# A two-block network on one core: layer norms that read their statistics from PSUM, and a state space stage with groups innermost and tiles taken in turn

## The reference

```python
bu_re = einsum('blgh,gph->lbgp', u, bb_re)          # 64 groups of 16 features, 64 states
bu_im = einsum('blgh,gph->lbgp', u, bb_im)
s_re, s_im = associative_scan(s_t = lbar * s_(t-1) + bu_t)
y = einsum('lbgp,ghp->blgh', s_re, c_re) - einsum('lbgp,ghp->blgh', s_im, c_im)
h = gelu(y + d_skip * x)
z = val(h @ w_glu) * sigmoid(gate(h @ w_glu));  mix = z @ w_out

h = layer_norm(ALPHA * h + mix, g, b)                # (x - mean) * rsqrt(var + eps) * g + b
h = layer_norm(ALPHA * h + swiglu_ffn(h), g2, b2)
```

## Time and profile before

| | |
|---|---|
| median of 3 runs | 2775.85 us (2774.55 to 2780.78) |
| the profiled execution | 2774.27 us, span from first to last instruction 2772.6 us |
| busy | PE 2511.0 us (91%), PEld 2037.5, DVE 1363.1 (49%), ACT 802.0, POOL 377.2 |
| mean granted TensorE clock | 0.966 of full speed |
| DMA | 210.20 MB, mean 76 GB/s |

### The profile page before, as it was taken

How to read it: one execution, slowest core, us unless ns; L and a number is a source line. 1 busy time by engine, 2 the same in 40 slices (tenths; PEclk the granted TensorE clock), 3 DMA queues, 4 the chain that set the end, 5 groups by cost and what they waited for, 6 DMA issues and landing times.

```text
span 2772.6 us, 31672 instructions
## 1 busy us (share of the span) xinstructions
PE 2511.0 (91%) x12367; PEld 2037.5 (73%) x12367; DVE 1363.1 (49%) x1587; ACT 802.0 (29%) x864; POOL 377.2 (14%) x254
## 2 busy tenths in 40 slices
PE   3359979999989998999997989899999998999999
PEld 2258768888868766788885866788787887788887
DVE  7983463333553566433355355554534435544443
ACT  3112232222231452322224245322322233222322
POOL 4920040000310005000032202100022000200000
PEclk9779999999999999999998999999999999999999
DMA  3042212322322001222233210232233220232232
GB/s 60 1 65 61 91 61 91 103 89 83 100 80 91 31 1 61 91 91 91 78 94 90 92 61 16 77 104 91 77 94 91 90 91 16 79 102 91 81 92 84
DMA packets 255936, 210.20 MB, mean 76 GB/s; under 512 B 12612, under 2 KB 253658, under 8 KB 255802
## 3 DMA queue, kind: packets, MB, share of 16 engines
q1 hardware_dynamic: 255018, 207.42, 24.6%
q0 software_dynamic: 848, 1.80, 0.4%
HBM read 204.75 MB, written 2.10 MB: 75 GB/s over the span
## 4 chain that ended last, share of the span: by engine, by line
PE 83%; DVE 10%; issue 2%; ACT 2%; SPq 1%; POOL 1%; DMA 0%; DVEq 0%; POOLq 0%; ACTq 0%
PE psum L753 14%; PE psum L755 14%; PE psum L754 14%; PE psum L784 9%; PE psum L785 8%; PE psum L786 8%; PE psum L868 2%; PE psum L870 2%; PE psum L869 2%; DVE residual L2017 1%; PE psum L739 1%; PE psum L708 1%; POOL tmp_a L523 1%; PE psum L904 1%; PE psum L922 1%
## 5 line engine op out<-in xcount | busy, mean ns | idle before, releaser
L1873 DVE TENSOR_TENSOR w_lo<-w_stage,w_hi 128x2048 fp32r<-128x2048 f32 x203 | 477.5, 2352 | 698.5 <-ACT w_hi L1286 698.5
L1286 ACT CAST w_hi<-w_stage 128x2048 fp32r<-128x2048 f32 x210 | 401.2, 1910 | 1403.1 <-PE psum L755 744.3
L784 PE MATMUL psum<-x_hi,w_hi 128*128 128x512 f32 x944 | 380.9, 403 | 71.8 <-DVE x_lo L2026 40.1
L785 PE MATMUL psum<-x_lo,w_hi 128*128 128x512 f32 x944 | 373.3, 395 | 0.0
L786 PE MATMUL psum<-x_hi,w_lo 128*128 128x512 f32 x944 | 372.6, 395 | 0.0
L753 PE MATMUL psum<-x_hi,w_hi 128*128 128x512 f32 x944 | 367.2, 389 | 0.0
L754 PE MATMUL psum<-x_lo,w_hi 128*128 128x512 f32 x944 | 367.2, 389 | 0.0
L755 PE MATMUL psum<-x_hi,w_lo 128*128 128x512 f32 x944 | 367.2, 389 | 0.0
L753 PE MATMUL psum<-hidden_hi,w_hi 128*128 128x512 f32 x832 | 325.4, 391 | 8.0 <-DVE w_lo L1873 2.9
L754 PE MATMUL psum<-hidden_lo,w_hi 128*128 128x512 f32 x832 | 323.8, 389 | 0.0
L755 PE MATMUL psum<-hidden_hi,w_lo 128*128 128x512 f32 x832 | 323.7, 389 | 0.0
(11 more groups left out here) (377 smaller groups left out, 3152.0 us busy)
## 6 DMA issues: line engine op xcount, KB each, us to landing
w_stage<-in_ffn_w_gu_dram SPq DMA_DIRECT2D x44, 1024.0 KB, 5.0
w_stage<-in_ffn_w_down_dram SPq DMA_DIRECT2D x64, 704.0 KB, 4.5
w_stage<-in_ffn_w_gate_dram SPq DMA_DIRECT2D x22, 1024.0 KB, 5.3
w_stage<-in_ffn_w_up_dram SPq DMA_DIRECT2D x22, 1024.0 KB, 5.3
w_stage<-in_sb_w_qkv_dram SPq DMA_DIRECT2D x12, 1024.0 KB, 5.0
w_stage<-in_od_w_in_dram SPq DMA_DIRECT2D x12, 1024.0 KB, 5.3
w_stage<-in_ev_w_in_dram SPq DMA_DIRECT2D x10, 1024.0 KB, 5.1
w_stage<-in_ssm_w_glu_dram SPq DMA_DIRECT2D x8, 1024.0 KB, 5.6
```

The costliest lines, as they stand in the source:

```text
L784: nc.tensor.matmul(bank[u], hi, xh[:, k, :], start=(k == 0), stop=False)
L785: nc.tensor.matmul(bank[u], hi, xl[:, k, :], start=False, stop=False)
L1286: nc.scalar.copy(whi[:, half, :], wst[:, half, :]).then_inc(whi_done, 1)
L1873: V.tensor_tensor(wlo[:, half, :], wst[:, half, :], whi[:, half, :].bitcast(F32), ALU.subtract).then_inc(wlo_done, 1)
```

## The change

Norms: the mean is no longer copied, and `mean` is bank 5 itself. ACT writes the reciprocal root into bank 6 (`rstd_all`), in the rms norms too. All eight chunks are centred by DVE, so that POOL goes from its sums straight to the last weight split. The order of DVE's steps changes: multiply chunk c, make `x_lo` of chunk c-1, centre chunk c+2. In norm 4 the mean square goes to bank 7.

State space stage: the input is copied unrounded (`x_f`), its `x_lo` is gone, and `ssm_out` takes the residual from `x_f` without rebuilding it. `toe` and `k_rows` are laid out with the group inside the time step, so that each DMA moves one contiguous run per partition. The matmuls of lines 708 and 739 are issued so that consecutive ones go to different tiles (four in turn), those of line 726 so that they alternate between two. Matmuls on different row halves go to different banks: banks are worked on in pairs, and the semaphores of a pair rise together. ACT now waits for all eight of POOL's `cl` rounds before its first copy to `k_rows` (before: ahead of its third), PE for six rounds before the first pair of line 708 and for eight before the second (before: five, six, seven, eight for the four banks).

```diff
+        mean, rstd_all = bank[5], bank[6]
-        mean, mean_sq, variance, rstd_ln = acc, tmp_c[:, 0, :], tmp_c[:, 1, :], tmp_b[:, 1, :]
+        mean_sq, variance, rstd_ln = tmp_c[:, 0, :], tmp_c[:, 1, :], tmp_b[:, 1, :]
-        toe = at("toeplitz", [P, GROUPS, P], hid_at + 36 * KB)
+        toe = at("toeplitz", [P, 4, TAU, 16, GH], hid_at + 36 * KB)
-        k_rows = at("k_rows", [P, 16, P], tmp_at + 8 * KB)
+        k_rows = at("k_rows", [P, TAU, 16, GH], tmp_at + 8 * KB)
+        x_f = at("x_feat", [P, DC, SEQ], xhi_at)
...
-                eng.dma_start(toe[s * GH:(s + 1) * GH, (q // 2) * 32 + q % 2:(q // 2) * 32 + 32:2, s * GH:P],
-                              k_rows[q * 32:q * 32 + GH, :, 0:P - s * GH]).then_inc(done, 16)
+                eng.dma_start(toe[s * GH:(s + 1) * GH, q, s:TAU, :, :],
+                              k_rows[q * 32:q * 32 + GH, 0:TAU - s, :, :]).then_inc(done, 16)
...
-                pool.wait_ge(ln_m2, 2 * n + 2)
-
-                pool.wait_ge(dev_sq, (n + 1) * DC)
-                for c in range(4, DC):
-                    sum_link(nc.gpsimd.tensor_tensor(res[:, c, :], res[:, c, :], mean, ALU.subtract))
                 split_last(n)
...
-            for b in range(4):
-                pe.wait_ge(w_ready, 4 + b + 1)
-                for q in range(4):
+            for b0 in (0, 2):
+                pe.wait_ge(w_ready, 4 + b0 + 2)
+                for swap in range(2):
                     for s in range(4):
-                        g = (q // 2) * 32 + 2 * (b * 4 + s) + q % 2
-                        j, half = g // 2, (g % 2) * 64
                         for ri, w in enumerate((w_re, w_im)):
-                            mm = nc.tensor.matmul(bank[4 + b][q * 32:q * 32 + 32, s * P:(s + 1) * P],
-                                                  bb[half:half + 64, ri, :, j], w[half:half + 64, j, 0:TAU, :], start=(ri == 0), stop=(ri == 1))
-                mm.then_inc(k_done, 1)
+                            for q in range(4):
+                                b = b0 + ((q % 2) ^ swap)
+                                g = (q // 2) * 32 + 2 * (b * 4 + s) + q % 2
+                                j, half = g // 2, (g % 2) * 64
+                                mm = nc.tensor.matmul(bank[4 + b][q * 32:q * 32 + 32, s * P:(s + 1) * P],
+                                                      bb[half:half + 64, ri, :, j], w[half:half + 64, j, 0:TAU, :],
+                                                      start=(ri == 0), stop=(ri == 1))
+                mm.then_inc(k_done, 2)
...
-            for b in range(8):
-                for g, dst in y_parts(b):
-                    j, half = g // 2, (g % 2) * 64
+            for b0 in range(0, 8, 2):
+                for s in range(4):
                     for ri, w in enumerate((w_re, w_im)):
-                        mm = nc.tensor.matmul(dst, states[half:half + 64, 0:NCH, ri, j], w[half:half + 64, j, 1:LAGS, :],
-                                              start=False, stop=(ri == 1), skip_group_check=True)
-                mm.then_inc(y_done, 1)
-                if b >= 3 and b % 2 == 1:
-                    y_features(b - 3)
-                    y_features(b - 2)
+                        for b in (b0, b0 + 1):
+                            for hf in range(2):
+                                g, dst = y_part(b, s, hf)
+                                j, half = g // 2, (g % 2) * 64
+                                mm = nc.tensor.matmul(dst, states[half:half + 64, 0:NCH, ri, j], w[half:half + 64, j, 1:LAGS, :],
+                                                      start=False, stop=(ri == 1), skip_group_check=True)
+                mm.then_inc(y_done, 2)
+                if b0 >= 2:
+                    y_features(b0 - 2)
+                    y_features(b0 - 1)
...
-                nc.scalar.activation(mean_sq, bank[5], ACT.Square).then_inc(ln_m2, 1)
-                nc.scalar.copy(mean, bank[5]).then_inc(ln_m2, 1)
+                nc.scalar.activation(mean_sq, mean, ACT.Square).then_inc(ln_m2, 1)
...
-                nc.scalar.activation(rstd_ln, rstd_ln, ACT.Exp, scale=-0.5).then_inc(act_link, 1)
+                nc.scalar.activation(rstd_all, rstd_ln, ACT.Exp, scale=-0.5).then_inc(act_link, 1)
...
-            for f in range(DC):
-                dve.wait_ge(xhi_done, f + 1)
-                V.tensor_tensor(xlo[:, f, :].rearrange("p (c s) -> p s c", s=TAU),
-                                bank[f][:, :].rearrange("p (s c) -> p s c", s=TAU),
-                                xhi[:, f, :].bitcast(F32).rearrange("p (c s) -> p s c", s=TAU),
-                                ALU.subtract).then_inc(x_ready, 1)
+            V.memset(marks[:, 11:12], 0.0).then_inc(x_ready, DC)
...
+                for c in range(DC):
+                    dve.wait_ge(ln_xc, n * DC + c + 1)
+                    V.tensor_tensor(res[:, c, :], res[:, c, :], rstd_all, ALU.mult).then_inc(ln_n, 1)
+                    if n < 3 and c > 0:
+                        low(c - 1)
+                    if c + 2 < DC:
+                        centre(c + 2)
+                pass_split(n)
+                if n < 3:
+                    low(DC - 1)
```

More of the change, by code:

```diff
@@ L723, in _ @@
             for b in range(8):
[L724 to L726 removed]
+                for s in range(4):
+                    for hf in range(2):
+                        g, dst = y_part(b, s, hf)
+                        nc.tensor.matmul(dst.rearrange("p (t h) -> p t h", h=GH), uu[:, g, :], toe_of(g), start=(s == 0),
+                                         stop=False, skip_group_check=True)
             def y_features(n):
@@ L833, in mean_square @@
                 pe.wait_ge(ln_sq, sq_count(n) + c + 1)
-                nc.tensor.matmul(bank[5], ones_mean[:, :], sq[:, c % 2, :], start=first, stop=last).then_inc(ln_sq_used, 1)
+                nc.tensor.matmul(bank[7 if n == 4 else 5], ones_mean[:, :], sq[:, c % 2, :], start=first,
+                                 stop=last).then_inc(ln_sq_used, 1)
             def norm(n):
@@ L1938, in shift @@
                 for c in range(DC):
-                    V.scalar_tensor_tensor(res[:, c, :], bank[4], -1.0 / (2 * P * (1.0 if c < 4 else ALPHA)), res[:, c, :],
+                    before = x_f[:, c, :] if n == 0 and c >= 4 else res[:, c, :]
+                    V.scalar_tensor_tensor(res[:, c, :], bank[4], -1.0 / (2 * P * (1.0 if c < 4 else ALPHA)), before,
                                            ALU.mult, ALU.add).then_inc(ln_shifted, 1)
```

59 lines of the change are left out of this document (25 added, 34 removed).

## The result

The changed kernel takes **2728.12 us** in the median of 4 runs (2726.96 to 2729.36), the kernel before 2778.32 us in its 4 (2774.55 to 2782.95). The ratio is 0.982, with a 95% interval from 0.980 to 0.984. Forecast were 2724 us and a range from 2715 to 2739. The profiled execution took 2728.07 us, against 2774.27 before, so 46.2 us are to be found between the two traces.

What follows compares the result with a forecast made beforehand. PE was taken to bound the kernel, so its gaps counted. Norms 0 to 2 (22.8 us), norm 3 (7.1) and the state space stage (22.4) sum to 52.3 us off 2774.3, plus 1.6 for the median: 2724 us, range 2715 to 2739.

Steps and rivals of the forecast that it cites:

- Norms 0 to 2: PE's gap of 13.4 us ahead of each of these layer norms' first matmul shrinks by 7.6 us, 22.8 us in all.
- Norm 3: With DVE free of POOL, the train of chunks starts 7.1 us earlier and PE's 12.7 us wait shrinks by as much.
- The rms norms: They keep their 4.74 us stall and are costed at nothing, at most 2 us each.
- The state space stage: Products with the states start 7.5 us earlier and run 15.5 us shorter, less 0.6 us at the end: 22.4 us.
- Line 707 and the DMAs: Line 708 before the change, with toe's DMAs: their speed and layout hide behind the scan, price 0, at worst 2 us.
- The restart at 1.2 GHz: PE, idle before the products with the states, restarts at half speed for 3.2 us, losing 1.6 us.
- Two tiles at once: Products with the states never run more than two tiles at once: 109 ns a matmul, 2730 us; chance 0.14.
- Order without effect: Matmul order makes no difference to the products with the states: 15.5 us fall away, 2740 us; chance 0.07.
- Norms at half: Norms gain half, as POOL's split holds DVE elsewhere or ACT can't deliver: 15 us fewer, 2739 us; chance 0.08.
- Slower by a change of tile: Changing tile at each matmul stops PE loading weights beside a running matmul: 77 us for line 739, 2791 us; chance 0.03.
- Scan not held up by line 498: POOL's product doesn't stall the scan, or segment_powers' collision vanishes: 3 to 10 us more gain, 2714 to 2721; chance 0.03.
- Nothing happens: PE's waits shrink, but later waits take all of the gain; chance 0.03.

Runs made afterwards that it cites:

- stats_in_sbuf: Changed kernel with the norms' mean and root back in SBUF, POOL still without centring and DVE in its new order: 2728.07 us.
- pool_centres: Changed kernel with POOL again centring chunks 4 to 7, from an SBUF copy of the mean, DVE's operands staying in PSUM: 2734.66 us.
- order_alone: Changed kernel with mean and root in SBUF and POOL centring chunks 4 to 7, so only DVE's new order stays in the norms: 2757.59 us.
- row_pairs: Changed kernel with line 747 issued to the two row halves (two banks) in turn, not four tiles: 2733.53 us.
- column_pairs: Changed kernel with line 747 issued bank by bank, the two column halves in turn, not four tiles: 2740.39 us.
- response_serial: Changed kernel with line 707 in its old order, one tile at a time: 2725.34 us.
- skip_early_resp_serial: skip_early (changed kernel, POOL's x_natural product made early) with line 707 in its old order, one tile at a time: 2725.35 us.
- bank_by_bank: Changed kernel with line 747 in its old order, bank by bank and one tile at a time: 2763.09 us.
- skip_early: Changed kernel with POOL's product of x_natural and d_rows made out of place at 29 us, not beside the scan: 2719.37 us.

## Why the prediction was right

**The bound** was PE's gaps, and it was they that shrank: 31.0 us in the four norms.

**Norms 0 to 2**, priced at 7.6 us each, gave 7.9. The 0.3 us taken off for waits in the later chunks didn't occur as waits; about as much was lost in the clock after the gap. DVE's instructions took 0.68 us, the first matmul came 5.3 us after the variance. **Norm 3**: 7.1 predicted, 7.3 measured. The reason given, DVE and POOL blocking each other, holds with one addition. I treated the operand in PSUM and POOL's free time as one cause. With one of them alone the gap stays at 5.5 to 7.3 us (stats_in_sbuf, pool_centres), and the new order, which I had inside the same sum, is 1.2 us of it by itself (order_alone).

**The rms norms**, priced at nothing, kept their stall of 4.7 us; none moved the difference by more than 1.6 us.

**The state space stage**, 22.4 predicted, gave 22.8, with two misses that cancel. The start of the products came 9.1 us earlier, not 7.5: `segment_powers` was held up by two POOL instructions only (0.84 and 1.33 us), since POOL's rounds ended at 143.2 and not at 144.6, and the scan was done at 200.5 rather than 202.0. Line 747 gave 14.4 instead of 15.5.

Its rate came out near, 60 to 64 ns a matmul against 60 taken from line 687, but that is in good part luck. This is the row of the kernel before:

```profile
146.00 3.10 PE L687 MATMUL psum<-u_chunks,bl_rows 128*64 128x64 f32 x64
```

A matmul of line 687 streams 64 columns, one of lines 739 and 747 streams 128, and line 687 alternates between two tiles, not four. Two tiles in turn with 128 columns need 112 ns (row_pairs), or 98 by the estimate from column_pairs. The row did show that PE can take in matmuls this fast, which is how the prediction argues too; it didn't show what four tiles do. (The clock over line 687 was 0.64, not 0.62, so its rate is 61 ns and not 59.) Where the products start at full clock, response_serial has 122 records in 3.92 us (64 ns a matmul) and skip_early_resp_serial 128 in 3.85 (60 ns).

Line 707 and the DMAs were priced at 0, with 2 us lost at worst. They were hidden, and the price missed two things. The DMAs were taken at their old 27.6 us and took 22.5. And the quick order of line 707 makes the stage 2.1 us longer, by the pause that it leaves (response_serial). The restart at 1.2 GHz was under-priced: it lasts some 5.5 us and costs 2.3 (127 records in 6.37 us, against 122 in 3.92 at full clock), not 3.2 and 1.6. The tail was -0.6 as forecast.

The section "Instruction Overhead" of the Trainium skill's "TensorEngine Tiling (Array Packing)" states its 60 cycles for matmuls. The 100 ns a product, an estimate that counts the two loads as well, is refuted by the 64 measured; for the two matmuls alone the estimate would be 50 ns. By "Key Properties" on the same page of the Trainium skill, different tiles load and multiply in parallel. The trace agrees in part: four tiles in turn give three times the rate of one (64 ns against 194), not the four times that the prediction drew from it.

**Rivals.** Two tiles at once: refuted, that is what row_pairs does (112 ns). Order without effect: refuted, bank_by_bank. Norms at half: refuted, POOL's split is over at 366.0, 2.7 us ahead of the first `x_lo`. Slower by a change of tile: refuted, row_pairs. Scan not held up by line 498 (500 now): refuted, the stall is there with 10.03 us, and skip_early shows what it cost. Nothing happens: refuted by 46.2 us between the traces.

**What the sum missed** is the 6.6 us in the linear attention, 2,000 us behind the last edited instruction. Up to there the traces differ by 52.1 us, where the sum said 52.3. That they agree so closely is partly luck: norms and state space stage gave 53.8, and smaller losses and gains of the clock and the rms norms, none of them in the sum, take off 1.7. The profiled executions end 46.2 us apart, 6.1 less than the sum. The forecast is off by 4 only, since it put the median 1.6 us above the profiled execution, and the changed kernel's lies only 0.05 us above. That the 6.6 us come from the clock is shown by the windows. That the change of timing in front of it brings it about is only argued.

## What to carry to other kernels

Where two engines block each other, look at which instruction ends the wait and what lies beside it. Here either of two cures closed most of the gap. The second cure bought 0.6 to 1.8 us a norm on top where it was the operand in PSUM, and 8.9 us over four norms, with the waits and the slow clock behind the gap, where it was POOL's free time. A faster piece behind a longer one need not buy anything, and in this stage it cost 2.1 us: PE arrived early, idled, and began the next piece at half clock. So ask of each order of matmuls also how it starts after a pause. What is hidden can change with the next edit: once the scan was shorter (skip_early), the same quick order was worth 6.0 us. Then look for what holds up the bound itself; moving one 8.8 us product out of the scan's way gave 8.6 us, more than a third of the 22.8 that the whole state space half had given.

## What the runs showed of the hardware

- Matmuls of 64 x 64 with 128 columns in float32: 194 ns each on one tile at a time at full clock (before), 112 ns with two row halves in turn (row_pairs), 60 to 64 ns with four tiles in turn (after, skip_early_resp_serial). With 64 x 32 and eight tiles, where four follow in turn (line 707), 57 ns instead of 176. With 128 x 64, 64 columns and two tiles in turn (line 687), about 60.
- At 1.2 GHz after a pause, the same 256 records stayed at 1.2 GHz for 48 us when issued one tile at a time (bank_by_bank), but reached 2.4 GHz after 4.1 to 6.1 us when issued four tiles in turn. Coming at full clock, one tile at a time kept it at full clock for 22.5 us (line 707 in response_serial). In one trace each, two column halves in turn stayed slow for 27 us and two row halves in turn did not.
- After pauses of 6.9 to 17 us PE began line 747 at 1.2 GHz (eleven traces), after 1.2 us or none at 2.4 GHz (three traces).
- A stretch of identical instructions after the same wait of 3.7 us ran slow for 7 us or for 21 to 24. The clock's fall came 0.2 to 0.3 us before PE's start in the three short cases and 0.1 to 0.5 us after it in the eleven long ones.
- In the norms, DVE instructions with one operand in PSUM took 0.68 us beside POOL instructions of 1.3 to 4.5 us. With both in SBUF they were held until POOL's was done and ended 0.3 to 0.6 us after it (3.84, 4.70, 4.98 and 10.03 us).
